# A two-block transformer forward pass on one core: head scalings and rotations moved into the attention's first steps

## The chip, the cores and the metric

One NeuronCore of a Trainium2 chip runs the whole program. The metric is the device time of one execution in microseconds. TensorE is called PE below, VectorE DVE, ScalarE ACT and GpSimd POOL; SP issues the transfers of the weights.

## What is computed

The reference is a forward pass of two blocks over 256 tokens of width 1024, the first with a context of 256 more tokens. All is fp32.

```python
for l in range(DEPTH):                       # block one, DEPTH = 2
    mod = silu_c @ w_ada[l] + b_ada[l]       # likewise mod_c for the context
    h  = modulate(rms_norm(x,  norm1_g[l]), sh1, sc1)
    hc = modulate(rms_norm(xc, norm1_g[l]), csh1, csc1)
    qa, ka, va, qb, kb, vb, ga, gb = split_in_proj(h @ w_in[l])
    qb = rms_norm(qb, q_norm_g[l]); kb = rms_norm(kb, k_norm_g[l])
    ya = window_attention_latent(apply_rope(qa), apply_rope(ka), va, kac, vac, sink_a[l])
    yb = full_attention_latent(apply_rope(qb), apply_rope(kb), vb, kbc, vbc)
    x = x + gt1 * ((sigmoid(ga) * (ya @ w_pa) + sigmoid(gb) * (yb @ w_pb)) @ w_o)
    h2 = modulate(rms_norm(x, norm2_g[l]), sh2, sc2)
    x = x + gt2 * ((silu(h2 @ w_gate) * (h2 @ w_up)) @ w_down)
    # layer 0: the same for the context xc; layer 1 has no queries of the context
x = rms_norm(x, final_norm_g)
for l in range(2):                           # block two
    h = rms_norm(x, norm_w[l]); p = h @ w_in2[l]
    # a top-k latent attention with partial rotations, a stick-breaking attention
    # and a chunked mLSTM; three gated branches, merged, projected, added to x
```

## The kernel before, in words

**Weights.** Every weight passes through the chip once, as 504 transfers of 512 KB that SP issues in a fixed order into a ring of 7 slots (`SLOTS`, L22). A slot of a product's weights is split before use: ACT writes the rounded high part (L1471), DVE (L1876) or POOL (L1810) the remainder, into a ring of 4 pairs (`PAIRS`, L23). Each 128x128 block of a product is then three matmuls, high (L1051), high against the other operand's low part (L1052), low (L1053), with 512 tokens in block one's layer 0 and 256 from its layer 1 on. `pool_share` says which share of the splits goes to POOL.

**The order.** `walk` (L292) writes one list of steps, and the program of each engine runs through that list in its order; nothing reorders it. `linear`, `together` and `token` (L175, L193, L214) yield one block at a time, `fill(n)` takes n of them out of a queue of products to stand between the steps of an attention, `reserve` (L276) takes slots for tiles that are used later, and `prepare` (L128) places the splits of slots that have arrived. `together` uses slots that `reserve` had kept, `linear` takes its slot when it comes to it.

**Modulation.** The vectors `mod` of block one come from 24 chunks of the weight `w_ada` (`ada`, L242). A chunk is 4 slots used without a split: 8 matmuls (L1135), then their transposes (L1148), a sum with the bias on DVE (`modadd`, L1952 and L1954) and a copy on ACT (L1520). `ADA_AT` (L30) says in which stage which chunks stand: of layer 0's attention with its G products 6 to 11, of layer 1's norm 1 16 to 19, of its attention 20 and 21.

**Norms.** `norm_root` and `norm_tiles` (L321) make a norm's mean, its broadcast by PE, and then per tile two DVE instructions (L2041, L2070) and one of ACT between them. Chunks and the first products of the next stage stand between the tiles. With `later`, splits of further slots stand between the tiles too, on POOL.

**Attention of block one.** The products Q come first, with K's rotations and those of Q 0 to 3 between them. Then come 3 blocks of G, the mean of the query heads that are normalised (`hq`; a power on POOL, L1819, and three small DVE instructions to L1989), 5 blocks of G, and for heads 4 to 7 in turn a broadcast by PE (L1190), a scaling (`hscale`, L2078) and a rotation (`rope`, L2110 to L2116), with 2 or 3 blocks between. Only behind these stands the first score. A step i of the attention is S (L1226, maxima on DVE L2132), blocks, `turn` of step i-1 (scaling L2157, transposes by PE L1239, copies L2165), `exp` on ACT (L1618), blocks, and PV (L1257) of an earlier step.

**Block two.** After the norm of its layer 0, whose broadcast lies in PSUM bank 7, 8 rotations `rope X` of 128x256 stand between products, each with a `keep` behind it (L2053; it scales a tile of the residual by the final norm of block one, and reads bank 7). The token-major products SV come next.

## Time and profile before

| | |
|---|---|
| three runs | 1922.01, 1923.55, 1929.08 us, median 1923.55 us |
| the profiled execution | 1927.86 us, its span 1926.4 us |
| mean granted clock of PE in it | 0.984 |
| busy: PE | 1828.0 us, 95% of the span |
| busy: DVE, ACT, POOL | 1084.6, 871.2, 331.4 us |
| from and to HBM | 269.23 MB read, 1.05 MB written, 140 GB/s |

The profiled execution took 4.3 us longer than the median of the three. The span is the time from its first to its last instruction. The granted clock of PE is given as a share: 1 stands for its level of 2.4 GHz, and a window in which part of the time was spent at 1.2 GHz shows a mean between 0.5 and 1.

### The profile page before, as it was taken

Reading aid. Unit: us, or ns where it says so; the run is one execution under the profiler, and the core shown is the slowest. Engines: PE = TensorE matmul, PEld = TensorE weight load, DVE = VectorE, ACT = ScalarE, POOL = GpSimd, SP = SyncE. Lnnn points to the kernel's source line nnn. Section 1 sums busy time; section 2 is a strip of 40 time slices with the busy share of each in tenths; the row PEclk is TensorE's granted clock in tenths of the full one; section 3 lists DMA queues with packets and bytes.
Section 4 is the critical chain, followed back from the end, with each engine's and each line's share of the span. In section 5 each row is a group of like instructions: output and inputs, shape, how many; then the busy total and the mean of one; then the engine's idle time right before and its main releaser. Section 6 shows DMA issues by size and latency. Waiting matters only on the chain.

```text
span 1926.4 us, 30442 instructions
## 1 busy us (share of the span) xinstructions
PE 1828.0 (95%) x12330; PEld 1550.1 (80%) x12330; DVE 1084.6 (56%) x2113; ACT 871.2 (45%) x1518; POOL 331.4 (17%) x153
## 2 busy tenths in 40 slices
PE   6989999999999999998999999989999999899997
PEld 3765566867888888586788999987888999788897
DVE  5245656533111111446876656788756788875576
ACT  4214445433222222234564544546555554655553
POOL 0321222433444444320000000110001001000100
PEclk9999999999999999998999999999999999999999
DMA  9424411244223322544236665553433455433342
GB/s 376 151 90 164 154 44 55 88 146 182 98 88 102 105 89 98 173 177 164 67 111 218 208 188 196 176 173 134 132 122 130 148 191 167 141 132 121 123 151 77
DMA packets 76731, 272.26 MB, mean 141 GB/s; under 512 B 8240, under 2 KB 11568, under 8 KB 76592
## 3 DMA queue, kind: packets, MB, share of 16 engines
q1 hardware_dynamic: 74656, 266.37, 40.8%
q10 hardware_dynamic: 1936, 3.94, 0.5%
q8 instruction: 98, 1.61, 0.3%
q14 instruction: 41, 0.34, 0.1%
HBM read 269.23 MB, written 1.05 MB: 140 GB/s over the span
## 4 chain that ended last, share of the span: by engine, by line
PE 75%; DVE 12%; ACT 7%; issue 3%; DMA 2%; POOL 2%; SPq 0%; ACTq 0%; DVEq 0%
PE bank L1051 21%; PE bank L1053 20%; PE bank L1052 20%; DVE low L1876 4%; ACT high L1471 2%; PE bank L1226 2%; PE bank L1257 2%; DMA raw<-stream 2%; PE bank L1239 2%; PE bank L1135 1%; POOL low L1810 1%; DVE tmp L2353 1%; PE bank L1352 1%; DVE hx L2225 1%; POOL hsq L1819 0%
## 5 line engine op out<-in xcount | busy, mean ns | idle before, releaser
L1051 PE MATMUL bank<-h,high 128*128 128x256 f32 (+1 forms) x2208 | 715.9, 324 | 16.9 <-POOL low L1810 4.6
L1053 PE MATMUL bank<-h,low 128*128 128x256 f32 (+1 forms) x2208 | 690.0, 313 | 0.0
L1052 PE MATMUL bank<-h,high 128*128 128x256 f32 (+1 forms) x2208 | 689.8, 312 | 0.0
L1471 ACT ACTIVATE high<-raw 128x1024 fp32r<-128x1024 f32 x408 | 426.8, 1053 | 227.7 <-PE bank L1053 225.0
L1051 PEld LDWEIGHTS bank<-h,high 128*128 128x128 f32 x2208 | 419.2, 190 | 92.0 <-issue 49.7
L1876 DVE TENSOR_TENSOR low<-raw,high 128x1024 fp32r<-128x1024 f32 x286 | 355.9, 1251 | 160.3 <-ACT high L1471 159.4
L1053 PEld LDWEIGHTS bank<-h,low 128*128 128x128 f32 x2208 | 418.7, 190 | 26.4
L1052 PEld LDWEIGHTS bank<-h,high 128*128 128x128 f32 x2208 | 419.6, 190 | 22.8
L1810 POOL TENSOR_TENSOR low<-raw,high 128x1024 fp32r<-128x1024 f32 x122 | 294.7, 2422 | 542.2 <-ACT high L1471 542.1
L1920 DVE TENSOR_TENSOR gt<-bank,gt 128x512 f32<-128x512 f32 (+1 forms) x44 | 24.6, 558 | 190.0 <-PE bank L1053 183.8
L1819 POOL TENSOR_TENSOR few<-few,halves 128x2 f32<-128x2 f32 (+2 forms) x19 | 16.4, 862 | 657.2 <-DVE few L1980 657.2
L1051 PE MATMUL bank<-hid,high 128*128 128x512 f32 (+1 forms) x352 | 117.0, 332 | 0.0
L1052 PE MATMUL bank<-hid,high 128*128 128x512 f32 (+1 forms) x352 | 117.0, 332 | 0.0
L1053 PE MATMUL bank<-hid,low 128*128 128x512 f32 (+1 forms) x352 | 117.0, 332 | 0.0
L1914 DVE SCALAR_TENSOR_TENSOR xc<-bank,mod,xc 128x256 f32<-128x256 f32 x72 | 32.6, 481 | 142.6 <-PE bank L1053 142.6
L1665 ACT ACTIVATE hid<-gt 128x512 fp32r<-128x512 f32 (+1 forms) x44 | 23.1, 525 | 135.4 <-DVE gt L1920 135.4
L1135 PE MATMUL bank<-raw,silu_c 128*32 128x512 f32 x384 | 64.8, 661 | 19.9 <-DMA raw<-stream 19.5
L1053 PEld LDWEIGHTS bank<-hid,low 128*128 128x128 f32 x352 | 66.1, 188 | 6.9
L1051 PEld LDWEIGHTS bank<-hid,high 128*128 128x128 f32 x352 | 66.1, 188 | 6.8
L1052 PEld LDWEIGHTS bank<-hid,high 128*128 128x128 f32 x352 | 66.1, 188 | 6.8
L1831 POOL TENSOR_TENSOR z<-z,dqs 128x1024 f32<-128x1024 f32 x2 | 6.2, 3108 | 342.7 <-ACT dqs L1744 342.7
L2132 DVE TENSOR_REDUCE small<-bank 128x1 f32<-128x512 f32 (+1 forms) x96 | 54.9, 598 | 10.3 <-PE bank L1226 8.8
(313 smaller groups left out, 2752.1 us busy)
## 6 DMA issues: line engine op xcount, KB each, us to landing
raw<-stream SPq DMA_DIRECT2D x504, 512.0 KB, 3.4
xc<-x_in SPq DMA_DIRECT2D x1, 1024.0 KB, 5.5
xc<-ctx_in SPq DMA_DIRECT2D x1, 1024.0 KB, 7.8
cst<-consts ACTq DMA_DIRECT2D x1, 896.0 KB, 8.6
cst<-consts ACTq DMA_DIRECT2D x1, 704.0 KB, 7.0
ukw<-uk ACTq DMA_DIRECT2D x1, 512.0 KB, 6.1
uvw<-uv ACTq DMA_DIRECT2D x1, 512.0 KB, 6.8
out<-xc ACTq DMA_DIRECT2D x1, 512.0 KB, 2.9
```

What stands on the lines that cost most here:

```text
L1051: mm(dst, wh, xh, start=start, stop=False)
L1052: mm(dst, wh, xl, start=False, stop=False)
L1053: return mm(dst, wl, xh, start=False, stop=stop)
L1135: ins = mm(banks[b][g, :], silu_c[:, k, :], raw[:, block // BLK % SLOTS, at:at + 512], start=k < 4, stop=k >= 4)
L1226: mm(banks[b][:, 0:w], Q[l][head(g), 4 * b_ + j, t * P:(t + 1) * P], K[l][head(g), b_, keys], start=True, stop=True).then_inc(S["S"], 1)
L1239: ins = nc.tensor.transpose(banks[b][:, s * P:(s + 1) * P], p[:, s * P:(s + 1) * P], ident)
L1257: ins = mm(banks[7][head(g), j * P:(j + 1) * P], V[l][:, first + s, c:c + HD], probT[l][2 * (i % LAG[l]) + g][:, s * P:(s + 1) * P], start ...
L1471: do(high[:, i % PAIRS, :], raw[:, slot % SLOTS, :], ACTF.Copy).then_inc(S["hi"], 1)
L1810: tt(low[:, i % PAIRS, :], raw[:, slot % SLOTS, :], high[:, i % PAIRS, :].bitcast(F32), ALU.subtract).then_inc(S["lo_pool"], 1)
L1876: tt(low[:, i % PAIRS, :], raw[:, slot % SLOTS, :], high[:, i % PAIRS, :].bitcast(F32), ALU.subtract).then_inc(S["lo_dve"], 1)
L1914: ins = stt(out=xc[:, jj, c], in0=ps[:, c], scalar=mod[:, at, s:s + 1], in1=xc[:, jj, c], op0=ALU.mult, op1=ALU.add)
L2132: nc.vector.tensor_reduce(st[:, g:g + 1], ps[:, 0:w], AX.X, ALU.max, negate=True).then_inc(S["masked_max"], 1)
```

## The change

It has five parts. All is a matter of order, but for the shape of block two's rotations.

1. **Head norm.** The mean of `hq` comes after 2 blocks of G instead of 3, and 6 blocks follow. Broadcast, scaling and rotation 4 + i then stand inside attention step i, for i = 0 to 3, behind S; the number of blocks in these steps rises from 2 and 2 to 3 and 3 in layer 0, and from about 3 and 3 to 5 and 5 in layer 1. The exponential waits for the rotation of Q 3 alone.
2. **Chunks.** A sum `modadd` stands a chunk later in the norms. Chunks 18 and 19 move from norm 1 of layer 1 to its attention.
3. **Slots ahead.** Before each chunk in the Q and G products one slot is reserved for the next tile, so that it is loaded and split ahead of the chunk.
4. **Later splits.** In norms with `later`, the splits leave the tiles and POOL, and stand on DVE behind the last tile.
5. **Block two.** The rotations are done in pairs, 4 of 128x512 with both temporaries. The keeps move behind them into the SV products and read a copy of bank 7 that ACT makes (`rootcopy`).

```diff
--- before.py
+++ after.py
@@ -28,7 +28,7 @@
 ODD = 48
 
 ADA_AT = {("n1", 0): (), ("Q", 0): (4, 5), ("G", 0): (6, 7, 8, 9, 10, 11), ("n2", 0): (12, 13, 14, 15),
-          ("n1", 1): (16, 17, 18, 19), ("G", 1): (20, 21), ("n2", 1): (22, 23)}
+          ("n1", 1): (16, 17), ("G", 1): (18, 19, 20, 21), ("n2", 1): (22, 23)}
 ADA_FILL = (1, 2, 1)
 
 EARLY_FILL = ((9, 16, 6), (9, 9, 6))
@@ -253,18 +253,13 @@
             if k == KT - 1:
                 for before in self.uncollected:
                     self.step("adac", before)
-                    if not later:
-                        self.step("modadd", before)
-                if later:
-                    self.unadded += self.uncollected
+                self.unadded += self.uncollected
+                for _ in range(len(self.unadded) - later):
+                    self.step("modadd", self.unadded.pop(0))
                 self.step("adacopy", c)
                 self.uncollected = [c]
             if k % 4 == 3:
                 yield
-            if k % 4 == 3:
-                for before in self.unadded:
-                    self.step("modadd", before)
-                self.unadded = []
 
     def collect(self):
         for c in self.uncollected:
@@ -319,23 +314,22 @@
         o.prepare(max(ahead - 2, 0))
 
     def norm_tiles(m, tiles=range(KT), pieces=iter(()), products=iter(()), n=0, later=0):
-        share = o.pool_share
         for k in tiles:
             o.step("norm", m, k)
             if k > tiles[0]:
                 o.step("normlo", m, k - 1)
-            if k > tiles[0] and later:
-                o.pool_share = (1, 1)
-                o.prepare(1)
-                o.pool_share = share
-                later -= 1
             some(pieces, ADA_FILL[2])
-            if k == tiles[0] and later:
-                o.reserve(later)
             if k > tiles[0] + 1:
                 some(products, n)
         o.step("normlo", m, tiles[-1])
-        for _ in chain(pieces, products):
+        for _ in pieces:
+            pass
+        if later:
+            share, o.pool_share = o.pool_share, (0, 1)
+            o.reserve(later)
+            o.prepare(later)
+            o.pool_share = share
+        for _ in products:
             pass
         if tiles[-1] == KT - 1:
             o.hold = False
@@ -381,14 +375,15 @@
         def queries():
             pieces = [o.ada(c) for c in ADA_AT.get(("Q", l), ())]
             for j in range(1 - l, 8):
-                for k, _ in enumerate(o.linear("Q", l, j)):
+                for k, _ in enumerate(o.together([("Q", l, j)]) if o.kept else o.linear("Q", l, j)):
                     if k == KT // 2 and j > 4:
                         o.step("headmean", ("hq", l), j - 1)
                     if k == KT - 1 and j >= 4:
                         o.step("sq", ("hq", l), j)
                     yield
-                if j % 2:
-                    yield from pieces.pop(0) if pieces else ()
+                if j % 2 and pieces:
+                    o.reserve(1)
+                    yield from pieces.pop(0)
 
         o.filling.append(queries())
         o.step("rope", "K", l, 0)
@@ -405,21 +400,15 @@
         def fill():
             pieces = [o.ada(c) for c in ADA_AT["G", l]]
             for j in range(16):
-                yield from o.linear("G", l, j)
-                yield from pieces.pop(0) if pieces else ()
+                yield from o.together([("G", l, j)]) if o.kept else o.linear("G", l, j)
+                if pieces:
+                    o.reserve(1)
+                    yield from pieces.pop(0)
 
         o.filling.append(fill())
-        o.fill(3)
+        o.fill(2)
         o.step("mean", ("hq", l))
-        o.fill(7 if last else 5)
-        for j in range(4, 9):
-            if j < 8:
-                o.step("bcast", ("hq", l), j)
-                o.step("hscale", "hq", l, j)
-            if j > 4:
-                o.step("rope", "Q", l, j - 1)
-            if j < 8:
-                o.fill((3, 3, 2, 2)[j - 4] if last else (2, 2, 2, 4)[j - 4])
+        o.fill(6)
         o.step("few")
 
         pairs = [(b, t, j) for t in range(n // P) for b in range(2) for j in range(4)]
@@ -427,13 +416,17 @@
         for i in range(len(pairs) + lag):
             if i < len(pairs):
                 o.step("S", l, i, *pairs[i])
-            o.fill(2 if l == 0 else 3 - i % 2)
+            o.fill((3 if i < 4 else 2) if l == 0 else 5 if i < 4 else 3 - i % 2)
+            if i < 4:
+                o.step("bcast", ("hq", l), 4 + i)
+                o.step("hscale", "hq", l, 4 + i)
+                o.step("rope", "Q", l, 4 + i)
             if 1 <= i <= len(pairs):
                 o.step("turn", l, i - 1, *pairs[i - 1])
             if i < len(pairs):
                 o.step("exp", l, i, *pairs[i])
                 o.step("even", l, i, *pairs[i])
-            o.fill((1 if i % 4 == 3 else 2) if l == 0 else 3)
+            o.fill((3 if i < 4 else 1 if i % 4 == 3 else 2) if l == 0 else 5 if i < 4 else 3)
             if i >= lag:
                 b, t, j = pairs[i - lag]
                 o.step("PV", l, i - lag, b, t, j)
@@ -558,14 +551,14 @@
         o.fill(8)
         o.step("totok", l, 0)
         o.step("totok", l, 1)
-        for i, j in enumerate((1, 4, 5, 2, 6, 7, 8, 9)):
+        for j in (1, 4, 6, 8):
             o.step("rope", "X", l, j)
-            o.fill(4)
-            if not l:
-                o.step("keep", i)
+            o.fill(8)
         o.rest()
         o.pool_share = (0, 1)
-        o.run(o.token("SV", l, 2, 512))
+        for k, _ in enumerate(o.token("SV", l, 2, 512)):
+            if not l:
+                o.step("keep", k)
 
         def projections():
             for j in range(8):
@@ -955,8 +948,9 @@
         def rope_of(name, l, j):
 
             if name == "X":
-                x = X[l][:, j, :] if j < 6 else DQS[l][:, j - 6, :]
-                return x, SWAP16, sign[:, 1:2], const("cos2"), const("sin2")
+                x = X[l][:, j:j + 2, :] if j < 6 else DQS[l][:, j - 6:j - 4, :]
+                cos, sin = (const(c).unsqueeze(1).to_broadcast([P, 2, SEQ]) for c in ("cos2", "sin2"))
+                return x, SWAP16, sign[:, 1:2], cos, sin
             x = (K if name == "K" else Q)[l][:, j, 0:SEQ]
             return x, SWAP64, sign[:, 0:1], const("cos1", 0, SEQ), const("sin1", 0, SEQ)
 
@@ -1207,7 +1201,7 @@
                                      r[:, t * g + i:t * g + i + 1].to_broadcast([P, P // g]), ident, start=True, stop=True)
                     ins.then_inc(S["bcast"], 1)
                     if m[0] == "nf":
-                        freed[b] = ("kept", KT)
+                        freed[b] = ("scaled", norm_no(("nw", 0), KT - 1))
                     elif m[0][0] != "h":
                         freed[b] = ("scaled", norm_no(m, KT - 1))
                     elif m[0][:2] == "hm":
@@ -1576,6 +1570,8 @@
                 elif kind == "rootcopy":
                     l = key[0]
                     act.wait_ge("bcast", no["bcast", ("nw", 1) if l else ("nf", 0)])
+                    if not l:
+                        do(lat[1][:, :], banks[7][:, 0:SEQ], ACTF.Copy)
                     do(lat[0][:, :], banks[7][:, 0:SEQ] if l else banks[7][:, SEQ:ALLT], ACTF.Copy).then_inc(S["roots"], 1)
 
                 elif kind == "norm":
@@ -1607,7 +1603,7 @@
                 elif kind == "exp":
                     l, i, b_, t, j = key
                     (_, w), st, at = keys_of(t), stat(l, i), 2 * no[step] - 1
-                    act.wait_ge("rope", no["rope", "Q", l, 7])
+                    act.wait_ge("rope", no["rope", "Q", l, 3])
                     for g, b in enumerate(bank_of["S", l, i, b_, t, j]):
                         if i >= 2:
                             act.wait_ge("turn", at + g - 4)
@@ -2050,7 +2046,7 @@
                 elif kind == "keep":
                     k = key[0]
                     dve.wait_ge("scaled", norm_no(("nw", 0), KT - 1))
-                    stt(out=xc[:, k, 0:SEQ], in0=xc[:, k, 0:SEQ], scalar=vector("gf", k), in1=banks[7][:, 0:SEQ],
+                    stt(out=xc[:, k, 0:SEQ], in0=xc[:, k, 0:SEQ], scalar=vector("gf", k), in1=lat[1][:, :],
                         op0=ALU.mult, op1=ALU.mult).then_inc(S["kept"], 1)
 
                 elif kind == "normlo":
@@ -2095,17 +2091,22 @@
                         rot = const("rot16" if name == "X" else "rot64")
                         nc.vector.tensor_reduce(signs, rot, AX.X, ALU.add).then_inc(S["signs"], 1)
                         dve.wait_ge("signs", 2 if name == "X" else 1)
-                    swapped, kept = (tmp[no[step] % 2][:, i * SEQ:(i + 1) * SEQ] for i in range(2))
+                    at = 1 if name == "Q" and j >= 4 else no[step] % 2
+                    swapped, kept = (tmp[at][:, i * SEQ:(i + 1) * SEQ] for i in range(2))
+                    if name == "X":
+                        swapped, kept = (t.rearrange("p (j t) -> p j t", t=SEQ) for t in tmp)
                     if name == "K" and j == 1:
                         dve.wait_ge("hscale", no["hscale", "hk", l, 1])
                     elif name == "Q" and j >= 4:
                         dve.wait_ge("hscale", no["hscale", "hq", l, j])
                     elif name == "X" and j >= 6:
-                        dve.wait_ge(*drained["DQ", l, j - 6])
+                        dve.wait_ge(*drained["DQ", l, j - 5])
+                    elif name == "X":
+                        dve.wait_ge(*drained["X", l, j + 1])
                     else:
                         dve.wait_ge(*drained[name, l, j])
-                    if no[step] > 2:
-                        dve.wait_ge("rope", no[step] - 2)
+                    if no[step] > 1:
+                        dve.wait_ge("rope", no[step] - 1)
                     own += 1
                     nc.vector.stream_shuffle(swapped, x, swap).then_inc(S["dve_own"], 1)
                     tt(kept, x, cos, ALU.mult).then_inc(S["rope_cos"], 1)
```

The hunks left out change only which number some of PE's waits name.

PE's order, layer 0, around the broadcasts of the query heads (L1190, which is L1184 after the change). Before:

```order
L1053 MATMUL bank<-h,low 128x512
L1190 MATMUL bank<-cst,hsq 64x128 x8
L1135 MATMUL bank<-raw,silu_c 32x512 x8
L1148 MATMUL bank<-cst,ada_part 128x128 x4
L1190 MATMUL bank<-cst,hsq 64x128 x8
L1051 MATMUL bank<-h,high 128x512
L1052 MATMUL bank<-h,high 128x512
L1053 MATMUL bank<-h,low 128x512
```

After (L1045 to L1047 are the product's matmuls, L1129 the chunk's, L1142 its transposes, L1220 the scores):

```order
L1047 MATMUL bank<-h,low 128x512
L1220 MATMUL bank<-K,Q 128x512 x2
L1129 MATMUL bank<-raw,silu_c 32x512 x8
L1142 MATMUL bank<-cst,ada_part 128x128 x4
L1045 MATMUL bank<-h,high 128x512
L1046 MATMUL bank<-h,high 128x512
L1047 MATMUL bank<-h,low 128x512
L1184 MATMUL bank<-cst,hsq 64x128 x8
```

The first scores now stand ahead of the chunk and of every broadcast, and a block stands between the chunk and the first broadcast.

DVE's order, layer 1, from the rotation of query tile 6 to the first maxima. Before:

```order
L2116 TENSOR_TENSOR Q<-tmp 128x256
L1876 TENSOR_TENSOR low<-raw,high 128x1024 x3
L1952 TENSOR_REDUCE mod<-bank 128x8
L1954 TENSOR_TENSOR mod<-mod,vec 128x8
L2110 STREAM_SHUFFLE tmp<-Q 128x256
L2111 TENSOR_TENSOR tmp<-Q,cst 128x256
L2113 SCALAR_TENSOR_TENSOR tmp<-tmp,small,cst 128x256
L2116 TENSOR_TENSOR Q<-tmp 128x256
L2127 TENSOR_TENSOR bank<-bank,cst 128x128
L2132 TENSOR_REDUCE small<-bank 128x1
L2127 TENSOR_TENSOR bank<-bank,cst 128x128
L2132 TENSOR_REDUCE small<-bank 128x1
```

After (L1872 is the split, L2133 the maxima, L2074 the scaling, L2166 the copy of the transposed probabilities), around the scaling of query tile 7, the last of the four:

```order
L2140 TENSOR_TENSOR small<-small,small_sink 128x2
L2142 TENSOR_TENSOR small<-small,small_sink 128x2
L1872 TENSOR_TENSOR low<-raw,high 128x1024 x3
L1948 TENSOR_REDUCE mod<-bank 128x8
L1950 TENSOR_TENSOR mod<-mod,vec 128x8
L2074 SCALAR_TENSOR_TENSOR Q<-Q,small,bank 128x256
L2111 STREAM_SHUFFLE tmp<-Q 128x256
L2112 TENSOR_TENSOR tmp<-Q,cst 128x256
L2114 SCALAR_TENSOR_TENSOR tmp<-tmp,small,cst 128x256
L2117 TENSOR_TENSOR Q<-tmp 128x256
L2166 COPY probT_1<-bank 128x512
```

Before, three splits, a sum and a rotation stood ahead of the first maxima of the attention. Now three splits, a sum, a scaling and a rotation stand between the maxima and the copy of the attention's third turn.

DVE's order, block two, layer 0, from its last rotations on. Before:

```order
L2116 TENSOR_TENSOR dqs<-tmp 128x256
L2053 SCALAR_TENSOR_TENSOR xc<-xc,vec,bank 128x256
L2110 STREAM_SHUFFLE tmp<-dqs 128x256
L2111 TENSOR_TENSOR tmp<-dqs,cst 128x256
L2113 SCALAR_TENSOR_TENSOR tmp<-tmp,small,cst 128x256
L2116 TENSOR_TENSOR dqs<-tmp 128x256
L2053 SCALAR_TENSOR_TENSOR xc<-xc,vec,bank 128x256
L1876 TENSOR_TENSOR low<-raw,high 128x1024 x5
```

After (L2049 is the keep):

```order
L2111 STREAM_SHUFFLE tmp<-dqs 128x512
L2112 TENSOR_TENSOR tmp<-dqs,cst 128x512
L2114 SCALAR_TENSOR_TENSOR tmp<-tmp,small,cst 128x512
L2117 TENSOR_TENSOR dqs<-tmp 128x512
L1872 TENSOR_TENSOR low<-raw,high 128x1024
L2049 SCALAR_TENSOR_TENSOR xc<-xc,vec,lat 128x256
L1872 TENSOR_TENSOR low<-raw,high 128x1024
L2049 SCALAR_TENSOR_TENSOR xc<-xc,vec,lat 128x256 x2
L1872 TENSOR_TENSOR low<-raw,high 128x1024
L2049 SCALAR_TENSOR_TENSOR xc<-xc,vec,lat 128x256 x2
L1872 TENSOR_TENSOR low<-raw,high 128x1024
```

The keep no longer stands behind each rotation, and the splits stand between the keeps instead of five in a row.

## Rows read from the trace of the kernel before

**Rows 1.** The page, part 4: shares of the chain that ended last, by engine.

```profile
PE 75%; DVE 12%; ACT 7%; issue 3%; DMA 2%; POOL 2%; SPq 0%; ACTq 0%; DVEq 0%
```

**Rows 2.** Windows: us, then PE, PEld, DVE, ACT, POOL busy (x), PEclk, DMA share, GB/s.

```profile
60.00:80.00 20.00, 17.33 (x97) 12.70 (x96) 2.98 (x10) 4.16 (x7) 6.32 (x3) 0.91 0.41 154
120.00:140.00 20.00, 14.89 (x108) 9.11 (x107) 8.79 (x19) 2.14 (x3) 6.34 (x2) 0.83 0.37 131
220.00:240.00 20.00, 18.14 (x107) 12.07 (x106) 11.18 (x25) 7.60 (x19) 3.56 (x2) 0.83 0.25 83
880.00:900.00 20.00, 13.16 (x84) 7.75 (x83) 16.39 (x42) 7.70 (x12) 0.00 (x0) 0.85 0.74 290
900.00:920.00 20.00, 20.00 (x157) 16.58 (x158) 16.59 (x39) 11.80 (x29) 0.00 (x0) 0.90 0.17 54
1040.00:1060.00 20.00, 16.76 (x120) 13.27 (x113) 10.68 (x23) 9.05 (x16) 2.99 (x2) 0.91 0.63 236
```

**Rows 3.** Timeline of PE, layer 0's Q stretch: start, us, what, [idle before <- releaser].

```profile
73.67 0.47 PE L1051 MATMUL bank<-h,high 128*128 128x512 f32 x1 [2.29 <-POOL low L1810]
86.39 1.92 PE L1135 MATMUL bank<-raw,silu_c 128*32 128x512 f32 x16
90.62 0.47 PE L1051 MATMUL bank<-h,high 128*128 128x512 f32 x1 [1.72 <-POOL low L1810]
```

**Rows 4.** Timeline of PE, layer 0's head norm and first scores.

```profile
116.46 0.39 PE L1053 MATMUL bank<-h,low 128*128 128x512 f32 x1
116.69 0.39 PE L1051 MATMUL bank<-h,high 128*128 128x512 f32 x1
126.98 1.98 PE L1190 MATMUL bank<-cst,hsq 128*64 128x128 f32 x16 [5.11 <-DVE hsq L1989]
128.89 3.64 PE L1135 MATMUL bank<-raw,silu_c 128*32 128x512 f32 x16
143.17 1.13 PE L1226 MATMUL bank<-K,Q 64*128 64x512 f32 x4 [0.78 <-ACT gates L1492]
```

**Rows 5.** Timeline of POOL and DVE, the same head norm.

```profile
118.62 5.41 POOL L1819 TENSOR_TENSOR hsq<-hsq,halves 128x32 f32<-128x32 f32 x1 [18.18 <-DVE hsq L1980]
124.07 2.32 DVE L1984 SCALAR_TENSOR_TENSOR hsq<-hsq 128x32 f32<-128x32 f32 x1 [5.53 <-POOL hsq L1819]
```

**Rows 6.** Windows of layer 0: a hscale with its rotation; an attention step.

```profile
136.80:139.40 2.60, 2.60 (x25) 1.90 (x23) 2.24 (x6) 0.00 (x0) 0.00 (x0) 1.00 0.94 373
163.80:169.30 5.50, 5.32 (x40) 3.64 (x38) 4.16 (x12) 2.03 (x6) 0.00 (x0) 1.00 0.83 334
```

**Rows 7.** Timeline of POOL, DVE and PE behind chunk 11.

```profile
213.87 7.31 POOL L1810 TENSOR_TENSOR low<-raw,high 128x1024 fp32r<-128x1024 f32 x3 [0.49 <-ACT high L1471]
216.79 2.09 DVE L1954 TENSOR_TENSOR mod<-mod,vec 128x8 f32<-128x8 f32 x1
218.94 0.66 PE L1239 MATMUL bank<-cst,prob 128*128 128x128 f32 x4 [2.17 <-DVE mod L1954]
222.15 1.97 PE L1257 MATMUL bank<-probT,V 128*64 128x128 f32 x16 [1.86 <-DVE probT L2165]
```

**Rows 8.** Timeline of PE, norm 2 of layer 0.

```profile
432.61 1.05 PE L1135 MATMUL bank<-raw,silu_c 128*32 128x512 f32 x4 [1.22 <-DMA raw<-stream]
```

**Rows 9.** Window of norm 1 of layer 1.

```profile
805.50:831.20 25.70, 21.87 (x106) 11.84 (x106) 17.56 (x38) 11.17 (x23) 4.85 (x2) 1.00 0.84 309
```

**Rows 10.** Timeline of DVE and PE, opening of layer 1's attention.

```profile
887.28 3.50 DVE L1876 TENSOR_TENSOR low<-raw,high 128x1024 fp32r<-128x1024 f32 x3
896.97 2.07 PE L1226 MATMUL bank<-K,Q 64*128 64x512 f32 x2 [6.84 <-ACT prob L1618]
```

**Rows 11.** Timeline of PE, norm 2 of layer 1.

```profile
1050.08 0.39 PE L1051 MATMUL bank<-h,high 128*128 128x256 f32 x1 [1.83 <-DVE h L2070]
```

**Rows 12.** Timeline of PE, block two, layer 0.

```profile
1290.05 0.50 PE L1051 MATMUL bank<-high,h 128*128 128x512 f32 x1 [1.89 <-DVE low L1876]
1297.91 0.50 PE L1051 MATMUL bank<-high,h 128*128 128x512 f32 x1 [2.08 <-DVE low L1876]
```

6 lines of the change are left out of this document (3 added, 3 removed).

## The prediction

> **What bounds the kernel now.** I read the chain of waits first: PE holds 75% of it, DVE 12%, ACT 7% [rows 1]. So the kernel lives on PE's work, and what an edit of the order can win is the time in which PE stands idle, plus the time in which it works at 1.2 GHz. The list of PE's waits then says where the idle time lies; I looked each large one up in the timeline. Last I took the granted clock by windows of 20 us. A window with mean c spent 40 x (1 - c) us at 1.2 GHz: 3.6 us in 60:80, 6.8 in 120:140 and 220:240, 6.0 in 880:900, 4.0 in 900:920, 3.6 in 1040:1060 [rows 2]. Each of these stretches begins at or in an idle stretch of PE: behind 2.29 us at 73.67 [rows 3], in the 5.11 us ahead of 126.98 [rows 4], behind 2.17 and 1.86 us at 218.94 and 222.15 [rows 7], in the 6.84 us ahead of 896.97 [rows 10], behind 1.83 us at 1050.08 [rows 11]. What to see in them: a wait costs its length, and often half of the work behind it again. The idle 1.72 us at 90.62 [rows 3] is of the same kind and shows no such drop in the rows read here.
>
> The profiled execution took 1927.86 us, 4.3 more than the median of 1923.55. All terms are read in it; I take their sum from the median.
>
> **The change, part by part.**
>
> *Slots ahead in the Q stretch.* A tile's split by POOL starts now only behind the chunk and ends late: 2.29 and 1.72 us [rows 3]. With a slot reserved, the split runs beside the chunk, which takes 1.92 us [rows 3], and the products before it. The waits go, and half of 3.6 us of slow clock: 2.29 + 1.72 + 1.8 = **5.8 us**. SP issues one transfer earlier and none more; of the ring of 7 slots one is held longer. I found no place where the transfers become late and cost that at nothing. If they did, PE would wait for the transfer as at 432.61 [rows 8], 1.2 us a time.
>
> *Head norm and first scores, layer 0.* Before, the power on POOL (5.41 us) and a small DVE instruction of 2.32 us [rows 5] run on while PE has only five blocks, 0.23 us a matmul, 0.69 a block [rows 4]. PE idles 5.11 us, and then does 8 broadcast matmuls twice in 1.98 us and a chunk in 3.64 us at the lower level [rows 4], against half of 1.98 and 1.92 us. That is 5.1 + 1.0 + 1.7 = 7.8 us. After, PE's order has six blocks (4.1), the first scores, the chunk (1.92), its transposes and one block (0.69) ahead of the first broadcast: 6.7 us and a little. The chain is 5.41 + 2.32 and two small instructions, 8.1 us. Between 0 and 1.4 us is left of the wait; I take 0.4. New is what the moved steps do inside the attention. A scaling with its rotation is 2.24 us of DVE, an attention step has 5.32 us of PE and 4.16 of DVE in 5.5 [rows 6]. With two blocks and a broadcast more a step has about 7.3 us of PE against 6.4 of DVE. So DVE fits, but the scaling of turn 0 and the rotation stand in one row. I take one wait of 2.24 - 0.69 = 1.6 us at the first turn, and half a block (0.35) at the three others: 3.0 with the 0.4. Bounds: 0, if the blocks cover all, and 4 x 2.24 = 9, if they cover nothing. Net **4.8 us**.
>
> *Behind chunk 11.* Three splits of POOL take 7.31 us, a sum over 128x8 takes 2.09 us beside them, and PE waits 2.17 and 1.86 us [rows 7]; with half of 6.8 - 1.2 us of slow clock this is 6.8 us. After the change one of the burst's four splits goes ahead of the chunk. I take a quarter, **1.7 us**; the ends are -2, if the sum now meets a turn's scaling, and 6.8.
>
> *Norm 2, layer 0.* The slot comes a step earlier, and the last long wait for a transfer goes: **1.2 us** [rows 8].
>
> *Norm 1, layer 1.* In this window PE works 21.87 of 25.7 us [rows 9]. The chunks 18 and 19 cost PE the same in the attention, so only idle time counts. With 8 transfers fewer to wait for and no split of POOL beside DVE, 0.3 of the 3.8 us stay: **3.5 us**.
>
> *Opening of layer 1's attention.* Three splits of 3.50 us, a sum and a rotation stand ahead of the first maxima, and PE waits 6.84 us for the exponentials. From 896.97 on it works at the lower level: 4.0 us in window 900:920 and 3.0 in the one before, half of which is 3.5 [rows 2, 10]. Together 10.3. After, DVE's order has the same three splits between the maxima and the copy of turn 2. With a scaling and a rotation (about 2) they are 5.5 us, against five blocks (half of 0.69 each at 256 tokens) and a chunk: 3.6. I take 2.7 us of wait there with the ACT steps, 1.8 for the other three turns, 0.9 of slow clock: 5.4. Two blocks fewer are left to cover the steps behind the attention: 0.7. Net 10.3 - 5.4 - 0.7 = **4.2 us**; ends 0 and 9.
>
> *Norm 2, layer 1.* The wait behind DVE goes with POOL's split beside it: 1.83 + 1.8 of slow clock = **3.6 us** [rows 2, 11].
>
> *Block two.* The waits 1.89 and 2.08 us for splits [rows 12] end rows of rotations and keeps on DVE. Paired rotations and keeps behind them bring these splits forward: **4.0 us**. ACT's extra copy lies beside splits of DVE. In layer 1 the pairs hide nothing that PE waits for: 0.
>
> *POOL beside DVE in the new steps.* The 128x32 instruction took 2.32 us while POOL split [rows 5], the 128x8 one 2.09 [rows 7]. Layer 0's opening now holds four splits of POOL and rotations with two operands in SBUF. I take a third of 4 x 2.1: **-2.8 us**; ends 0 and -8.4. The Trainium skill, "SBUF — State Buffer", section "Who interferes with whom", says that a DVE instruction with two SBUF inputs and a GpSimd instruction that reads SBUF exclude each other and that whoever issues first holds the shared pair. The two rows agree with it, and it speaks against this part of the change: by it alone every rotation behind a split would wait, and the term would be its end of -8.4.
>
> Sum: 5.8 + 4.8 + 1.7 + 1.2 + 3.5 + 4.2 + 3.6 + 4.0 - 2.8 = **26.0 us**, so 1923.55 - 26.0 = **1897.5 us**.
>
> **The rivals.**
>
> *B, the openings give back what they win.* DVE and ACT, not the head norm, pace the first steps. Then the terms 4.8, 1.7 and 4.2 are zero, and 15.3 us remain: 1908.3 us. For it: DVE is busy 16.4 of 20 us around 890 [rows 2], and gets no less work. Against: six to ten blocks a step.
>
> *D, nothing is left.* Each of the 8 opening steps loses 2 us more, about one scaling with rotation. 15.3 - 16 is -0.7, some 1924 us. It needs the blocks to cover nothing, which the step of 5.5 us with 5.32 of PE [rows 6] speaks against.
>
> *C, slower: PE stays at 1.2 GHz through both openings.* Short waits in every step, with bursts of matmuls between, keep the level down as at 126.98 and 896.97 [rows 4, 10]. The 8 steps hold some 8 us of PE's work each, and at half speed cost 64 us more: 1923.55 - 26.0 + 64, about 1961 us. It decides from 26 us of work at the lower level; from 36 on the kernel is measurably slower. A step before has gaps of 0.2 us in 5.5 at level 1.00 [rows 6], which speaks against it. The Trainium skill, "TensorE: Matmul & The Clock Gate", section "A second HAM failure mode: psum-queue depth-cycling", tells of a kernel whose short idles between groups of matmuls make the clock swing between its levels; no row here shows it for idles this short.
>
> **How the numbers follow.** The sum as worked out: 0.62. B 0.20, D 0.11, C 0.07. The range goes down to the ends of the openings (three terms better by 3.0, 5.1 and 3.4: 1886) and up past B to where D begins, 1912. A difference under 0.5%, 9.6 us, can hardly be told from none with this kernel. The first two cases are faster by more: 0.82. D is within it, 0.11, and C slower, 0.07.
>
> **What would show it.** In the profile after: no wait over 1 us for POOL's splits before 100 us; the wait for the broadcasts under 1.5 us and a chunk behind it in 1.9 instead of 3.6; no wait of 6.8 us in layer 1's opening, the windows there at 0.95 or more; norm 1 of layer 1 in about 17 us; no wait over 1 us for a split around block two's first rotations; the first four turns of each attention with waits of 0.3 to 2.7 us. Waits of 2 us at each of the eight turns would mean B or D, a clock near 0.5 over more than 20 us in an opening C. The forecast is also wrong if transfers become late where slots are held longer, with PE waiting for `stream` in the G products.

## The result, and the profile after

| | before | after |
|---|---|---|
| runs beside each other, median | 1925.26 us (4 runs) | 1898.12 us (4 runs: 1890.77, 1896.94, 1899.30, 1899.74) |
| ratio, 95% interval | | 0.9847, 0.9821 to 0.9873 |
| the same kernel sent again (E1 below), median | 1923.98 us (7 runs) | 1887.65 us (5 runs: 1886.44 to 1899.04) |
| ratio, 95% interval | | 0.9794, 0.9761 to 0.9827 |
| the profiled execution | 1927.86 us, span 1926.4 | 1890.77 us, span 1889.3 |

The change makes the kernel faster, by 27 us in the first comparison and by 36 us in the second. All executions seen in this study give a median of 1925.3 us for the kernel before (34) and 1892.8 us for the change (9), 32.6 us apart. The forecast was 26.0 us. The two profiled executions are 37.1 us apart, and the reason for these different numbers is a finding of its own, below.

The page of the changed kernel, its first part (busy time, share of the span, instructions) and the chain that ended last by engine, which answers to [rows 1]:

```profile
PE 1812.8 (96%) x12330; PEld 1542.3 (82%) x12330; DVE 1086.2 (57%) x2078; ACT 871.7 (46%) x1519; POOL 320.9 (17%) x148
...
PE 76%; DVE 12%; ACT 7%; issue 2%; DMA 1%; POOL 1%; DVEq 0%; SPq 0%; ACTq 0%
```

PE does the same 12330 matmuls in 15.2 us less busy time than before (1828.0 us), and the idle rest of the span falls from 98.4 to 76.5 us. Of the 15.2 us, 11.9 are the clock: PE spent 63.1 us at the lower level before and 39.3 us after, and half of the difference is lost work. The 21.9 us of idle time are the waits. The list of PE's waits (line waited for: us in total, times, longest), its largest:

```profile
PE bank L1129 <- DMA raw<-stream: 14.4, 5, 10.6
PE bank L1233 <- DVE mod L1950: 6.4, 3, 4.0
...
PE bank L1045 <- issue: 5.0, 2, 3.7
```

The wait of 6.8 us for exponentials, the one of 5.1 for the head norm and those for POOL's splits are gone from the list. In second place now are 6.4 us for the sum `mod` of a chunk (2.2 before); and "issue" has grown from 1.9 to 5.0 us. Windows of 20 us (us, then PE, PEld, DVE, ACT, POOL busy and instructions, granted clock, DMA share, GB/s), to be held against [rows 2]:

```profile
60.00:80.00 20.00, 19.63 (x114) 14.84 (x113) 2.98 (x10) 4.75 (x8) 6.39 (x3) 1.00 0.42 152
120.00:140.00 20.00, 19.40 (x136) 11.72 (x134) 17.14 (x46) 7.34 (x17) 2.62 (x2) 1.00 0.63 240
200.00:220.00 20.00, 15.98 (x96) 10.75 (x95) 13.46 (x23) 6.79 (x17) 6.43 (x3) 0.83 0.46 173
880.00:900.00 20.00, 20.00 (x170) 16.59 (x170) 14.48 (x30) 11.25 (x29) 0.00 (x0) 0.91 0.41 152
1020.00:1040.00 20.00, 19.80 (x174) 19.61 (x174) 15.37 (x25) 12.88 (x20) 0.00 (x0) 1.00 0.66 227
```

The Q stretch and the first opening run at 1.00 with PE at 19.6 and 19.4 us of 20 (before 0.91 and 0.83 with 17.3 and 14.9). The stretch behind chunk 11, now at 200 to 220, is still at 0.83. PE's timeline (start, us, what, idle time before and its releaser) at the first scores and at the three longest waits that are left between 100 and 960 us:

```profile
116.16 1.13 PE L1220 MATMUL bank<-K,Q 64*128 64x512 f32 x4
117.22 1.92 PE L1129 MATMUL bank<-raw,silu_c 128*32 128x512 f32 x16
120.69 1.09 PE L1184 MATMUL bank<-cst,hsq 128*64 128x128 f32 x16 [0.26 <-DVE hsq L1985]
...
206.80 1.12 PE L1233 MATMUL bank<-cst,prob 128*128 128x128 f32 x4 [4.02 <-DVE mod L1950]
...
315.82 0.77 PE L1045 MATMUL bank<-h,high 128*128 128x512 f32 x1 [3.71 <-issue]
...
879.48 1.09 PE L1233 MATMUL bank<-cst,prob 128*128 128x128 f32 x8 [2.08 <-DVE mod L1950]
```

The first scores come at 116.16, the chunk behind them takes 1.92 us instead of 3.64, and the broadcast waits 0.26 us instead of 5.11 [rows 4]. Behind chunks 11 and 21 and at the end of layer 0's attention PE waits 4.02, 2.08 and 3.71 us. POOL's and DVE's rows at the first and the last of these places tell why:

```profile
199.43 7.00 POOL L1806 TENSOR_TENSOR low<-raw,high 128x1024 fp32r<-128x1024 f32 x3 [11.79 <-ACT high L1465]
202.09 2.05 DVE L2140 TENSOR_TENSOR small<-small,small_sink 128x2 f32<-128x2 f32 x1
204.18 2.27 DVE L2142 TENSOR_TENSOR small<-small,small_sink 128x2 f32<-128x2 f32 x1
...
312.59 2.35 POOL L1806 TENSOR_TENSOR low<-raw,high 128x1024 fp32r<-128x1024 f32 x1 [6.89 <-ACT high L1465]
312.72 2.24 DVE L1950 TENSOR_TENSOR mod<-mod,vec 128x8 f32<-128x8 f32 x1
```

Two DVE instructions on 128x2 numbers take 2.05 and 2.27 us. Each ends just after one of POOL's three splits (7.00 us for three, from 199.43 on). The last sum of the modulation takes 2.24 us beside a single split.

**Where the time went.** The stretches below run from the start of one instruction of PE to that of the next one named, in the two profiled executions. The Q stretch's gain is without the one block that the change moves across its end (0.69 us, [rows 4]); the next stretch's is with it.

| stretch, up to | before | after | gain | forecast |
|---|---|---|---|---|
| mean of the query heads, layer 0 | 117.37 | 110.93 | 5.8 | 5.8 |
| last PV, layer 0 | 209.81 | 199.94 | 10.6 | 4.8 + 1.7 - 2.8 = 3.7 |
| norm 2, layer 0 | 95.08 | 97.64 | -2.6 | 0 |
| norm 1, layer 1 | 378.10 | 376.95 | 1.2 | 1.2 |
| first head mean (of the keys), layer 1 | 44.44 | 33.73 | 10.7 | this and the next two rows: |
| last PV, layer 1 | 138.08 | 134.24 | 3.8 | 3.5 + 4.2 = 7.7 |
| norm 2, layer 1 | 56.20 | 57.53 | -1.3 | |
| block two's first norm | 194.19 | 189.80 | 4.4 | 3.6 |
| block two's second norm | 346.41 | 342.39 | 4.0 | 4.0 |
| end | 346.7 | 346.2 | 0.5 | 0 |
| sum | | | 37.1 | 26.0 |

Two chunks move from the fifth stretch to the sixth, and two blocks from the seventh to the sixth, so the three are read together: 13.2 us against 7.7. The openings won more than forecast; one place lost 2.6 us where nothing was expected.

### The profile page after: what moved, and what is told of

Read it like the earlier page. It is cut to its first block, busy times and chain, and to the rows that moved or that the text cites. A ratio compares the mean times of both kernels' runs of the same rounds, so it can differ in the third digit from the quotient of the medians.

```text
span 1889.3 us, 30389 instructions
## 1 busy us (share of the span) xinstructions
PE 1812.8 (96%) x12330; PEld 1542.3 (82%) x12330; DVE 1086.2 (57%) x2078; ACT 871.7 (46%) x1519; POOL 320.9 (17%) x148
## 3 DMA queue, kind: packets, MB, share of 16 engines
HBM read 269.23 MB, written 1.05 MB: 143 GB/s over the span
## 4 chain that ended last, share of the span: by engine, by line
PE 76%; DVE 12%; ACT 7%; issue 2%; DMA 1%; POOL 1%; DVEq 0%; SPq 0%; ACTq 0%
PE bank L1045 22%; PE bank L1047 21%; PE bank L1046 21%; DVE low L1872 3%; ACT high L1465 2%; PE bank L1251 2%; PE bank L1220 2%; PE bank L1129 2%; PE bank L1233 2%; DMA raw<-stream 1%; DVE tmp L2354 1%; PE bank L1346 1%; DVE hx L2226 1%; POOL few L1815 0%; ACT L1691 0%
## 5 line engine op out<-in xcount | busy, mean ns | idle before, releaser
L1045 PE MATMUL bank<-h,high 128*128 128x256 f32 (+1 forms) x2208 | 713.3, 323 | 13.5 <-issue 5.0
L1047 PE MATMUL bank<-h,low 128*128 128x256 f32 (+1 forms) x2208 | 687.3, 311 | 0.0
L1045 PEld LDWEIGHTS bank<-h,high 128*128 128x128 f32 x2208 | 416.9, 189 | 85.3 <-issue 44.0
L1872 DVE TENSOR_TENSOR low<-raw,high 128x1024 fp32r<-128x1024 f32 x291 | 364.9, 1260 | 158.8 <-ACT high L1465 158.1
L1047 PEld LDWEIGHTS bank<-h,low 128*128 128x128 f32 x2208 | 416.8, 189 | 26.2
L1806 POOL TENSOR_TENSOR low<-raw,high 128x1024 fp32r<-128x1024 f32 x117 | 284.2, 2435 | 526.9 <-ACT high L1465 526.9
L1045 PE MATMUL bank<-hid,high 128*128 128x512 f32 (+1 forms) x352 | 117.0, 333 | 0.0
L1047 PE MATMUL bank<-hid,low 128*128 128x512 f32 (+1 forms) x352 | 117.0, 332 | 0.0
L1910 DVE SCALAR_TENSOR_TENSOR xc<-bank,mod,xc 128x256 f32<-128x256 f32 x72 | 32.6, 481 | 143.3 <-PE bank L1047 142.8
L1129 PE MATMUL bank<-raw,silu_c 128*32 128x512 f32 x384 | 58.5, 642 | 14.5 <-DMA raw<-stream 14.4
L1047 PEld LDWEIGHTS bank<-hid,low 128*128 128x128 f32 x352 | 66.1, 188 | 6.9
L1045 PEld LDWEIGHTS bank<-hid,high 128*128 128x128 f32 x352 | 66.1, 188 | 6.8
L1626 ACT ACTIVATE probT<-bank 128x512 f32<-128x512 f32 (+1 forms) x48 | 25.2, 524 | 92.5 <-PE bank L1233 92.5
```

The source lines that it names most:

```text
L1045: mm(dst, wh, xh, start=start, stop=False)
L1047: return mm(dst, wl, xh, start=False, stop=stop)
L1129: ins = mm(banks[b][g, :], silu_c[:, k, :], raw[:, block // BLK % SLOTS, at:at + 512], start=k < 4, stop=k >= 4)
L1626: do(probT[l][2 * (i % LAG[l])][:, 0:w], banks[bank_of[step][0]][:, 0:w], ACTF.Copy).then_inc(S["turned_act"], 1)
L1806: tt(low[:, i % PAIRS, :], raw[:, slot % SLOTS, :], high[:, i % PAIRS, :].bitcast(F32), ALU.subtract).then_inc(S["lo_pool"], 1)
L1872: tt(low[:, i % PAIRS, :], raw[:, slot % SLOTS, :], high[:, i % PAIRS, :].bitcast(F32), ALU.subtract).then_inc(S["lo_dve"], 1)
```

## The experiments

Stretches are those of the table. Each experiment undoes or alters one part of the changed kernel ("the change" below); its profiled execution is held against that of the change.

One trace tells a stretch only so far. From norm 2 of layer 0 to norm 1 of layer 1 the change and the twelve runs below took 375.4 to 378.3 us, though only E6 edits anything there. The stretch up to the keys' head mean in layer 1, unedited in E2 and E7, took 35.23 us in both, with one fall of the clock of 3.4 us in it, and 33.74 in the change, with none. So a difference of 1.5 us in one stretch, and of 3 us in the longest ones, is not told from none where only the length says so.

**E1, the change again.** No edit.

> The changed kernel once more. Its profiled execution took 1890.77 us and its other three 1896.94 to 1899.74, so 6 to 9 us are not in that trace. Theory: the extra time lies in the first 430 us, where POOL splits beside DVE (the 4.02 us wait behind chunk 11 and the 3.71 us one at the attention's end), since which of the two engines starts first differs from execution to execution; this run's trace should then differ from the first one by over 3 us there and by under 1 us behind norm 1 of layer 1. Rival: the granted clock differs throughout, and the difference is spread over the whole span.

Measured: median 1887.65 us of five, the profiled execution 1899.04 us with a span of 1897.6, 8.3 us more than the first one. The theory falls: up to block one's last norm the stretches agree within 0.6 us each. The rival falls too, since the mean clock is 0.99 in both. 7.8 us lie in a single stretch, from norm 2 of layer 1 to block two (197.57 against 189.80 us), where PE idles 0.7 us in the one and 1.8 in the other and the clock never falls. The same window of it, of the first execution of the change:

```profile
1050.00:1070.00 20.00, 20.00 (x179) 20.00 (x178) 12.45 (x16) 9.48 (x14) 0.00 (x0) 1.00 0.63 208
```

and of this one:

```profile
1050.00:1070.00 20.00, 20.00 (x172) 20.00 (x171) 11.55 (x14) 10.14 (x15) 0.00 (x0) 1.00 0.53 182
```

PE is busy all of the 20 us at clock 1.00 in both, and does 179 matmuls in one and 172 in the other. The starts of its matmuls on 256 tokens are 113 ns apart in the one and 118 ns in the other, for the whole feed-forward part. In the other twelve traces, of the kernel before and of E2 to E12, the feed-forward part is at 113 ns. In the stretch ahead of it (merge and output products of layer 1) the change was at 118 ns in both executions, and so were E4, E11 and E12; the kernel before and the other runs were at 113. That pace is the -1.3 us of the table: 445 matmuls, six fewer than before, take longer with about the same idle time (3.6 against 3.3 us).

**E2, the old head norm.**

```diff
-        o.fill(2)
+        o.fill(3)
         o.step("mean", ("hq", l))
-        o.fill(6)
+        o.fill(7 if last else 5)
+        for j in range(4, 9):
+            if j < 8:
+                o.step("bcast", ("hq", l), j)
+                o.step("hscale", "hq", l, j)
+            if j > 4:
+                o.step("rope", "Q", l, j - 1)
+            if j < 8:
+                o.fill((3, 3, 2, 2)[j - 4] if last else (2, 2, 2, 4)[j - 4])
...
-            if i < 4:
-                o.step("bcast", ("hq", l), 4 + i)
-                o.step("hscale", "hq", l, 4 + i)
-                o.step("rope", "Q", l, 4 + i)
```

The numbers of blocks in the first four steps are the old ones too (2 and 2, about 3 and 3).

> The change without its first part: mean behind 3 blocks, then all scalings and rotations ahead of the first scores. Theory (openings gain): layer 0 from the mean of the query heads to the last PV takes some 9 us more than the 199.9 us of the changed kernel, with a wait of about 5 us for the head norm and a chunk at the lower clock; layer 1's stage some 5 to 8 us more with a wait of 5 us or more ahead of the second scores; about 1913 us. Rival B (openings give it all back): within 2 us of 1898. If the forecast's sizes were right it would be 1898 + 4.8 + 4.2 = 1907.

Measured: 1900.18 us (4 runs), against 1887.65 for the change beside it, so 12.5 us more; the profiled spans differ by 8.0. From the mean to the last PV of layer 0 it takes 207.23 us, with the moved block 8.0 more than the change; in layer 1's attention 138.23, 4.0 more although six blocks fewer (0.35 us each) lie in it, so 6.1. The waits are back where they were:

```profile
121.23 1.98 PE L1188 MATMUL bank<-cst,hsq 128*64 128x128 f32 x16 [5.10 <-DVE hsq L1989]
...
874.50 1.72 PE L1224 MATMUL bank<-K,Q 64*128 64x512 f32 x2 [2.88 <-ACT prob L1618]
```

5.10 us for the head norm and 2.88 for the exponentials, the latter less than half of the 6.84 before. The sizes by stretch are near the theory's 9 and 5 to 8 us; the wait in layer 1 is shorter than its 5 us, and the whole, 1900, less than its 1913. Rival B, that the openings give everything back, is out: this part alone is worth 8.0 and 6.1 us there.

But the next stretch, to norm 2 of layer 0, takes 95.02 us here, as in the kernel before, and 97.64 in the change. The last modulation sum comes 2.11 us behind the start of POOL's split here, and 0.13 in the change:

```profile
318.59 2.35 POOL L1810 TENSOR_TENSOR low<-raw,high 128x1024 fp32r<-128x1024 f32 x1 [6.27 <-ACT high L1469]
320.70 0.27 DVE L1954 TENSOR_TENSOR mod<-mod,vec 128x8 f32<-128x8 f32 x1
```

It takes 0.27 us instead of 2.24: in both it ends just after the split. So 2.6 of the 8.0 us are lost again behind layer 0's attention, by where that one sum falls, and the part is worth 5.4 us in layer 0.

**E3, no slot ahead.**

```diff
-                yield from o.together([("G", l, j)]) if o.kept else o.linear("G", l, j)
-                if pieces:
-                    o.reserve(1)
-                    yield from pieces.pop(0)
+                yield from o.linear("G", l, j)
+                yield from pieces.pop(0) if pieces else ()
```

and the same in `queries`.

> The change without slots reserved ahead of the chunks. Theory: the waits of 2.29 and 1.72 us for POOL's splits in the Q stretch come back, with 3.4 us of slow clock: 5.8 us there; and behind chunk 11 the burst has four splits again, 1 to 2 us more: about 1905 us. Rival: only the Q stretch's waits come back and the burst behind chunk 11 costs no more or less than now: 1904. Rival 2, the slot ahead does nothing and the waits went for another reason: 1898.

Measured: 1901.61 us (4 runs). The Q stretch is 53.54 us long, 5.9 more, with the two old waits:

```profile
73.95 0.47 PE L1042 MATMUL bank<-h,high 128*128 128x512 f32 x1 [2.29 <-POOL low L1803]
89.25 0.47 PE L1042 MATMUL bank<-h,high 128*128 128x512 f32 x1 [1.72 <-POOL low L1803]
```

Behind chunk 11 PE waits 5.49 instead of 4.02 us, with four splits in the row; that attention takes 1.8 us more. In layer 1's attention it is 4.7 us more, with a new wait of 1.51 us for a split of DVE, and one of 2.80 for the sum of chunk 21 instead of 2.08. The forecast had looked for the slot's worth in layer 0 alone.

**E4, two slots ahead of the last chunk.**

```diff
-                    o.reserve(1)
+                    o.reserve(1 if len(pieces) > 1 else 2 - len(o.kept))
```

> The change with two slots reserved ahead of the last chunk of each attention, so that no row of three splits follows it. Theory (the row of splits is what waits): the waits of 4.02 us behind chunk 11 and of 2.08 us behind chunk 21 fall under 1 us, and 6.8 us and 3.4 us of slow clock with them: 4 + 3 + 2 + 1.5, about 10 us less, 1888 us. Rival (POOL beside small DVE instructions is what waits, in a row or not): POOL's splits stand elsewhere and meet other DVE instructions there; layer 0 gains under 2 us, only layer 1 gains its 3: 1894.

Measured: 1891.44 us (4 runs), span 1884.9. Behind chunk 21 the longest wait is 0.94 us. Behind chunk 11 a wait of 1.92 us is left, and DVE's rows there show which instruction it is:

```profile
202.16 2.05 DVE L2140 TENSOR_TENSOR small<-small,small_sink 128x2 f32<-128x2 f32 x1
204.24 0.16 DVE L2142 TENSOR_TENSOR small<-small,small_sink 128x2 f32<-128x2 f32 x1
```

With two splits in the row only the first of the two small instructions stands behind POOL; the second takes its 0.16 us. Layer 0's attention is 4.1 us shorter. The attention of layer 1 is not (134.05 against 134.24), although its wait is over 1 us shorter. The median is 3.8 us above that of the change beside it (1887.65) and 1.3 below that of all nine executions: by the medians nothing is won, and the gain stands on the traces alone. So both readings were half right: the length of the row decides how many small instructions are caught, and POOL catches one also in a short row.

**E5, chunks 18 and 19 back in the norm.**

```diff
-          ("n1", 1): (16, 17), ("G", 1): (18, 19, 20, 21), ("n2", 1): (22, 23)}
+          ("n1", 1): (16, 17, 18, 19), ("G", 1): (20, 21), ("n2", 1): (22, 23)}
```

> The change with chunks 18 and 19 back in norm 1 of layer 1. Theory (the norm waits for transfers): PE idles there 3 to 4 us more, waiting for `stream`, and the stretch from the norm to the head mean of layer 1 grows by 3.5 to 5.6 us beyond the chunks' own 5.2 of PE's work; the attention gets 5.2 us shorter and no better otherwise: 3.5 to 5.6 us in all. Rival (chunks were also cover in the attention): the attention gets shorter by less than 5.2, since its four opening steps lose two chunks to stand behind; over 6 us in all.

Measured: 1895.60 us (2 runs). The norm's stretch takes 5.8 us more, 0.6 beyond the chunks' own work on PE (1.92 + 0.66 us each, 5.2 for two). PE's idle time in it is 2.9 us, against 2.8 in the change, so the theory of 3 to 4 us more waiting falls. The attention holds two chunks less and four blocks more, 3.8 us less of PE's work, and takes 1.0 us more:

```profile
870.30 1.50 PE L1233 MATMUL bank<-cst,prob 128*128 128x128 f32 x8 [2.42 <-DVE mod L1950]
880.05 0.66 PE L1233 MATMUL bank<-cst,tmp 128*128 128x128 f32 x4 [1.13 <-DVE Q L2074]
```

PE waits 2.42 and 1.13 us in the opening steps, against 0.3 and 2.08 in the change. The rival came true: in an opening a chunk is cover for DVE, and the two chunks cost the attention nothing. Of the 0.6 + 4.8 us that the move is worth only 0.6 lie in the norm. From its start to that of the next block a chunk takes 2.27 us (117.22 to 119.49 in the change); counted so, the two shares are 1.3 and 4.1. The profiled spans differ by 3.7 us, since the next stretch has the four blocks less and runs at the 113 ns pace here.

**E6, splits between the tiles on POOL again.** `norm_tiles` as before the change.

> The change with the splits of the norms between the tiles on POOL again. Theory: in norm 2 of layer 1 the wait of 1.83 us for DVE and 3.4 us of slow clock come back, 3.6 us, 1 us in norm 2 of layer 0, and 1 to 2 in norm 1 of layer 1, since a DVE instruction with two inputs in SBUF stands behind each of POOL's splits: 5 to 7 us. Rival: the waits there were for transfers, and nothing comes back but in norm 2 of layer 1: under 3 us.

Measured: 1900.03 us (2 runs). Norm 1 of layer 1 takes 3.5 us more, norm 2 of layer 0 0.7, which is inside the scatter, and the stretch from norm 2 of layer 1 6.1. At the last, POOL, DVE and PE:

```profile
1021.80 2.36 POOL L1807 TENSOR_TENSOR low<-raw,high 128x1024 fp32r<-128x1024 f32 x1 [7.22 <-ACT high L1466]
1020.82 0.48 DVE L2067 SCALAR_TENSOR_TENSOR h<-tmp,mod,h 128x256 fp32r<-128x256 f32 x1 [2.89 <-ACT h L1596]
1022.16 2.29 DVE L2067 SCALAR_TENSOR_TENSOR h<-tmp,mod,h 128x256 fp32r<-128x256 f32 x1 [0.34 <-ACT h L1596]
1024.88 0.48 DVE L2067 SCALAR_TENSOR_TENSOR h<-tmp,mod,h 128x256 fp32r<-128x256 f32 x1
1024.50 0.58 PE L1046 MATMUL bank<-h,high 128*128 128x256 f32 x1 [1.83 <-DVE h L2067]
```

The DVE instruction at 1022.16 stands behind POOL's split, 2.29 us instead of 0.48. PE's wait of 1.83 us is followed by 6.8 us at the lower clock. In norm 1 of layer 1 the 3.5 us are a wait for the same DVE instruction, here behind two splits of POOL in a row:

```profile
798.95 0.79 PE L1046 MATMUL bank<-h,high 128*128 128x512 f32 x1 [3.34 <-DVE h L2067]
```

It isn't the wait of the kernel before, which was for transfers (2.55 and 0.45 us at 809.60 and 819.41). With the chunks back and the splits late (E5) the waits for transfers are 1.25 us. E5 and E6 together say that the place of the splits, and of the slots reserved for them, is worth most of the norm's gain, and the chunks' move little of it; why the waits for transfers got shorter isn't shown.

**E7, the keeps between the paired rotations.**

```diff
-        for j in (1, 4, 6, 8):
+        for i, j in enumerate((1, 4, 6, 8)):
             o.step("rope", "X", l, j)
-            o.fill(8)
+            o.fill(4)
+            if not l:
+                o.step("keep", 2 * i)
+            o.fill(4)
+            if not l:
+                o.step("keep", 2 * i + 1)
```

> The change with the keeps back among block two's rotations, which stay in pairs; the keeps read the copy of bank 7. Theory (pairs alone free DVE enough): the waits of 1.89 and 2.08 us stay away, under 1 us is lost. Rival (the row of five splits behind the keeps is what PE waited for): one of the two waits, about 2 us, comes back.

**E12, the rotations apart, with the keeps behind them.**

```diff
-        for j in (1, 4, 6, 8):
+        for j in (1, 4, 5, 2, 6, 7, 8, 9):
             o.step("rope", "X", l, j)
-            o.fill(8)
+            o.fill(4)
```

with `rope_of` and the rotation's waits as before the change, 8 of 128x256.

> The change with block two's rotations apart again, 8 of 128x256; the keeps stay behind them, in the SV products. Together with the run that had the keeps between paired rotations this tells which of the two edits wins the 4.0 us between block two's two norms. There the keeps between brought one wait of 1.6 us back and cost no time in the stretch (342.3 against 342.4 us). Theory (either edit alone frees DVE enough, since each takes away one of two things in front of the splits): the stretch stays within 1 us of 342.4. Rival (the pairs are what counts): waits of 1.9 us and more come back and the stretch takes 344 to 346 us. The other stretches should be those of the change.

Measured: E7 1892.03 us (2 runs), its stretch 342.32 us against 342.39; E12 1893.43 us (2 runs), 344.79. PE's waits for splits in E7, and in E12:

```profile
1257.81 0.50 PE L1048 MATMUL bank<-high,h 128*128 128x512 f32 x1 [1.57 <-DVE low L1875]
```

```profile
1257.45 0.50 PE L1044 MATMUL bank<-high,h 128*128 128x512 f32 x1 [0.79 <-DVE low L1871]
1263.81 0.50 PE L1044 MATMUL bank<-high,h 128*128 128x512 f32 x1 [0.58 <-DVE low L1871]
...
1286.68 1.42 PE L1304 MATMUL bank<-tmp,cst 128*128 128x384 f32 x2 [3.50 <-DVE tmp L2252]
```

In E7 one wait of 1.57 us came back, but a later one of 2.64 us (at 1283.12 in the change) is 2.46 long and the window 1280 to 1300 is at 1.00 instead of 0.91; so the stretch hides what the keeps cost. In E12 the waits for splits are small, but the one for `tmp` further on is 3.50 instead of 2.64 us. These three make 2.2 us. The theory of E12 falls, and its rival has the time right and the waits wrong: it looked for waits of 1.9 us for splits. The pairs hold 2.4 of the 4.0 us. The keeps' share, up to 1.6 us, isn't settled by one trace.

**E8, on top of E4: the last split of layer 0's attention on DVE.**

```diff
+                if j == 14 and not l:
+                    o.pool_share = (0, 1)
...
         o.rest()
+        if not l:
+            o.pool_share = (1, 1)
```

> Two slots ahead of the last chunks, and the one split at the end of layer 0's attention on DVE instead of POOL. Theory (the 3.71 us wait there is the last modulation sum standing behind POOL's split, 2.24 us for 128x8): the wait falls to 1.7 us or less and the slow clock behind it from 6.8 to 3.4 us: 2 + 1.7 = 3.7 us less than with two slots ahead alone, in the stretch from the last PV to norm 2 of layer 0. Rival (the wait is ACT's and DVE's work on h itself): nothing changes, or DVE's split of 1.25 us adds to it.

Measured: 1885.09 us (5 runs). PE's wait is 4.11 us, not shorter; the stretch takes 97.26 us against 97.86 in E4. DVE's rows at the place:

```profile
310.05 1.22 DVE L1876 TENSOR_TENSOR low<-raw,high 128x1024 fp32r<-128x1024 f32 x1 [1.85 <-ACT high L1469]
311.30 0.87 DVE L2177 COPY Q<-bank 64x256 f32<-64x256 f32 x2
312.20 0.19 DVE L1952 TENSOR_REDUCE mod<-bank 128x8 f32<-128x32 f32 x1
312.43 0.17 DVE L1954 TENSOR_TENSOR mod<-mod,vec 128x8 f32<-128x8 f32 x1
```

The sum takes 0.17 us, so POOL's share of the old 3.71 us was there; but DVE's split of 1.22 us, and ACT's part of 1.05 us ahead of it, stand in front of the copies of Q, and cost as much. The theory named the instruction rightly and the cure wrongly.

**E9, on top of E4: the same split behind the work on h.**

```diff
-                yield from o.together([("G", l, j)]) if o.kept else o.linear("G", l, j)
+                yield from o.together([("G", l, j)]) if o.kept else o.linear("G", l, j, None, j == 15 and not l)
...
         if not last:
             for j in range(8):
                 o.step("hm", l, j)
+            o.hold = False
+            o.prepare()
```

> Two slots ahead, and the last split of layer 0's attention put behind the work on h instead of on another engine. In the trace before this one ACT's and DVE's parts of that split (1.05 and 1.22 us) stood in front of the copies of Q and the modulation sum, so moving it to DVE won nothing. Theory (whatever stands in front of this chain is waited for): the wait falls from 3.7 to 4.1 us to under 2 us, and the slow clock behind it from 6.8 to 3.4 or less: 3.5 us less than with two slots ahead alone. Rival (the chain itself, copies of Q, sums, h, is 3.5 us long): the wait stays over 3 us.

Measured: 1885.38 us (6 runs, 1878.03 to 1892.71), ratio to the kernel before 0.9784, 0.9755 to 0.9814; span 1877.3 at a mean clock of 0.996. The wait and a window around it:

```profile
310.05 0.47 PE L1047 MATMUL bank<-h,high 128*128 128x512 f32 x1 [1.90 <-issue]
```

```profile
300.00:320.00 20.00, 18.10 (x100) 13.92 (x97) 12.84 (x28) 14.24 (x29) 5.93 (x3) 1.00 0.17 53
```

The wait is 1.90 us and no fall of the clock follows; the stretch from the last PV takes 93.44 us, 4.4 less than with E4. In the profiled executions E9 is 12.0 us faster than the change, with the 113 ns pace in the feed-forward part of both. By the medians it is 7.4 us below the change's nine executions; its interval against the kernel before overlaps that of the change's second comparison, not that of the first. E8, without this gain in its trace, has the same median (1885.09), so the medians do not show the 4.4 us.

**E10, all splits of layer 0's attention on DVE.**

```diff
         o.filling.append(fill())
+        o.pool_share = (0, 1)
...
         o.rest()
+        if not l:
+            o.pool_share = (1, 1)
```

> The change with all splits of layer 0's attention on DVE, so that POOL holds no SBUF port there. Theory (the 4.02 us wait behind chunk 11 is two small DVE instructions of 128x2 that stood 2.05 and 2.27 us behind POOL's splits): DVE does the three splits in 3.7 us, the wait is about as long as in layer 1 (2.1 us), DVE instructions of 128x2 take 0.16 us everywhere, and the stretch from the head mean to the last PV takes 2 to 4 us less than 199.9. Rival (DVE, at 76% of a step, cannot take 16 splits of 1.25 us more): waits in other steps, the stretch grows by 5 us or more.

Measured: 1895.24 us (2 runs). The attention takes 203.72 us, 3.8 more. The small instructions take 0.16 us, and PE still waits, here and in many steps:

```profile
204.29 0.66 PE L1236 MATMUL bank<-cst,prob 128*128 128x128 f32 x4 [3.43 <-DVE mod L1953]
...
233.80 1.09 PE L1254 MATMUL bank<-probT,V 128*64 128x128 f32 x16 [2.01 <-DVE probT L2169]
```

In front of the first of these stand three splits in a row, 3.49 us on DVE. The theory falls, and the rival has the direction right (3.8 us, not 5 or more). POOL's splits are worth having although each may hold up DVE once.

**E11, the old number of blocks in the opening steps.**

```diff
-            o.fill((3 if i < 4 else 2) if l == 0 else 5 if i < 4 else 3 - i % 2)
+            o.fill(2 if l == 0 else 3 - i % 2)
...
-            o.fill((3 if i < 4 else 1 if i % 4 == 3 else 2) if l == 0 else 5 if i < 4 else 3)
+            o.fill((1 if i % 4 == 3 else 2) if l == 0 else 3)
```

> The change with the old number of blocks (2 and 2, or 3 and 3) in the four opening steps. Theory (the extra blocks are the cover of the moved scalings and rotations): a scaling with its rotation is 2.24 us of DVE in a step of 5.5 us with 4.16 of DVE; without two more blocks a step in layer 0 has 6.4 us of DVE against 5.9 of PE, so each of four steps waits 0.5 to 1.5 us, and in layer 1 more, where the fewer blocks are 0.35 us each: 2 to 6 us in layer 0, 4 to 10 in layer 1, partly won back by blocks left for the end. Rival (DVE has slack enough, the blocks only shift work): under 1 us in each.

Measured: 1889.71 us (2 runs). PE waits more in layer 0's opening:

```profile
120.64 1.09 PE L1184 MATMUL bank<-cst,hsq 128*64 128x128 f32 x16 [0.93 <-DVE hsq L1985]
...
129.89 0.65 PE L1233 MATMUL bank<-cst,prob 128*128 128x128 f32 x4 [0.76 <-DVE Q L2074]
...
147.06 0.66 PE L1233 MATMUL bank<-cst,prob 128*128 128x128 f32 x4 [0.75 <-DVE Q L2074]
149.47 1.09 PE L1251 MATMUL bank<-probT,V 128*64 128x128 f32 x16 [1.06 <-DVE probT L2166]
```

and 1.92, 1.00 and 0.76 us in layer 1's. The waits in layer 0's opening add up to 4.6 us, against 1.0 with the extra blocks, and in layer 1's to 3.7 against 2.4: the cover is real. But the two stretches from the head mean to norm 2 of layer 0 take 295.4 us together, 2.2 less than in the change, since with the blocks gone chunk 11 falls elsewhere, no row of three POOL splits meets the maxima, and the 4.02 us wait and its slow clock are not there. In layer 1 the attention loses 4.1 us beyond the 18 blocks that move (0.35 us each), and the stretch behind it, where they now cover, wins 5.0, with 0.6 instead of 3.6 us of idle time. The theory was right about the waits and wrong about the sum: the extra blocks won no time, in either layer or by the medians (1889.71 us against 1892.8 of the change's nine executions).

## Why the prediction was right, and where its steps were not

The measured median lies 0.6 us from the forecast of 1897.5, faster and inside the range, but that nearness is luck: all nine executions of the change have a median of 1892.8, 4.7 us lower, and in the profiled executions the gain was 37.1 us, 11 more than the sum. The upper end of the range takes 3.4 us for the opening of layer 1 where the term's own end of 9 gives 4.8. By its own steps:

- **Slots ahead in the Q stretch**, 5.8: measured 5.8, and 5.9 by E3. What the step left out is layer 1, where the slots ahead act by the same mechanism.
- **Head norm and first scores**, 4.8: measured 8.0 (E2). The 7.8 us taken off were about right: 5.11 + 1.98 + 3.64 became 0.26 + 1.09 + 1.92, 7.5 us less. The step that failed is the price of the new waits, 3.0 us ("one wait of 1.6 us at the first turn, and half a block at the three others"). The profile shows four waits of 0.26 us, 1.0 in all. The bound of 0 had been the nearer one, as the blocks cover DVE (4.6 us of waits without them, E11). What the step did not see is the 2.6 us behind the attention, which leave 5.4.
- **Behind chunk 11**, 1.7: measured about 0 for the waits and the clock there, 4.02 us and a window at 0.83 against 2.17 + 1.86 and 0.83. "I take a quarter" of the burst of four was the wrong rule. What counts is which small DVE instructions a row of POOL splits catches (E4, E11). The fourth split did cost 1.5 us in E3.
- **Norm 2 of layer 0**, 1.2: its stretch gained 1.2, but the waits for transfers are as long as before (1.28 and 0.38 us at 417.47 and 418.91, 0.42 and 1.22 before). The step that failed is "the last long wait for a transfer goes". The 1.2 us lie inside the scatter of this stretch, 375.4 to 378.3 us, and are no measured gain.
- **Norm 1 and opening of layer 1**, 3.5 + 4.2 = 7.7: measured 13.2, of it 5.5 in the norm (10.7 less the 5.2 of the chunks) and 7.7 behind it. Norm 1's gain is there, but by the splits taken from between the tiles (E6) more than by the chunks (0.6, E5). In the opening the wait behind three splits was forecast at 2.7 and is 2.08 us, the other three turns at 1.8 and are 0.3 in all. The step that failed is "the chunks 18 and 19 cost PE the same in the attention, so only idle time counts": there they are cover, worth 4.1 to 4.8 us (E5), and so are the slots ahead, worth 4.7 (E3).
- **Norm 2 of layer 1**, 3.6: measured 4.4, and 6.1 lost when the split is put back (E6). Mechanism and place as forecast.
- **Block two**, 4.0: measured 4.0, 2.4 of it by the pairs (E12); the two waits that the step named are gone.
- **POOL beside DVE**, -2.8: the mechanism is right and its place was not. PE waited for two instructions on 128x2 numbers behind chunk 11 (2.05 and 2.27 us) and for the last modulation sum (2.24 us), not for rotations with two operands in SBUF. Layer 0's opening had three splits of POOL, not four, and none met a rotation: its product with the cosine took 0.41 us all four times. A scaling of probabilities there did meet one (2.59 us instead of 0.48, at 152.42), and so did two such products in the Q stretch (2.35 and 2.05 us), and PE waited for none of them. The last sum cost 2.6 us in a stretch for which nothing was forecast: 3.71 instead of 1.90 us of wait and twice the slow clock. E9 won it back.

The rivals: B is out by E2, D by the stretches, and C too: the clock is at 1.00 in both openings but for 3.6 us in window 880:900, behind chunk 21. The rule of the Trainium skill, "SBUF — State Buffer", section "Who interferes with whom", agrees with E2, E4, E6 and E10: DVE instructions with both inputs in SBUF took 2.0 to 2.3 us when they met a POOL split near its start, 0.27 when they met its end, and without one 0.16 us on 128x2 and 0.48 on 128x256. The extreme that the prediction worked out from it, every rotation waiting, did not come about.

## What to carry to other kernels

A chain of small instructions that an engine must finish before the next matmul can be hidden by putting its links inside steps that have work of their own, if those steps have enough for the next matmul to do: two chunks as cover were worth over 4 us here (E5). Blocks taken from elsewhere shortened the waits but not the time (E11); count what moved work covers at its old place as well as at its new one. Where two engines hold each other up, as DVE and POOL here, look not at the large instructions that may collide, but at the few small ones that somebody waits for, and keep rows of splits away from them. A split placed in front of a chain that PE waits for cost about the same on either engine (3.71 and 4.11 us of wait); behind the chain the wait was 1.90 us.

## What the runs showed of the hardware

- PE showed two paces for back-to-back matmuls on 256 tokens at the same granted clock of 1.00: 179 or 172 in 20 us (E1). It kept one for a whole stretch; the feed-forward part of layer 1 took 7.8 us more of 190, 1.0 of it idle time. The pace differed between two executions of the same kernel; of the 14 traces, E1's alone had the slower one in this part. What sets it, and whether it is behind the other executions of the change at 1897 to 1900 us, isn't shown: only profiled executions show their pace.
- A DVE instruction on 128x2 numbers took 2.05 us beside a POOL split and 0.16 us without (E4). One on 128x8 took 2.24 us when it came 0.13 us behind the split's start, and 0.27 us 2.11 us behind it (the change, E2).
- Waits of 1.90 us passed without a fall of the clock in E9; waits of 2.08 us (chunk 21) and 1.83 us (E6) were each followed by one. The wait of 1.72 us in the Q stretch passed in the kernel before and was followed by 3.4 us at the lower level in E3. Behind chunk 11 a wait of 1.92 us passed without a fall in E4, and one of 1.91 was followed by 3.4 us at the lower level in E8. The wait of 4.0 us at that place was followed by 6.8 us in the change, E1, E5 and E7, and by 3.4 in E6 and E12. A wait's length alone does not tell whether the clock falls, or for how long.
